# Four filler products for nine ahead of the third modulation unit, and the first weight difference moved behind a convolution

## What is computed

```python
mod = jax.nn.silu(c) @ w_ada[l] + b_ada[l]
shift1, scale1, gate1, shift2, scale2, gate2 = jnp.split(mod, N_MOD, axis=-1)
h = modulate(rmsnorm(x, norm1_w[l]), shift1, scale1)
proj = h @ w_in[l]
r_q, r_k, r_v, r_g, d_q, d_k, d_v, d_z, d_a, d_b = jnp.split(proj, cuts, axis=-1)
...
ret = rmsnorm(ret).reshape(B, T, RET_WIDTH) * jax.nn.silu(r_g.astype(jnp.float32))
qkv = jax.nn.silu(causal_dwconv(jnp.concatenate([d_q, d_k, d_v], axis=-1), conv_w[l]))
...
dn = gated_delta_rule(dq, dk, heads(cv, DN_HEADS), g, beta)
...
x = x + gate1[:, None, :] * mix
ffn = hierarchical_moe(h2, ...)
```

## Time and profile before

| | |
|---|---|
| three runs | 912.74, 915.47, 915.58 us (median 915.47) |
| the profiled execution | 915.49 us |
| its span, first to last instruction | 913.7 us |
| mean granted clock of PE | 0.994 of full speed |
| busy: PE, DVE, ACT, POOL | 98%, 46%, 36%, 13% |
| DMA over the span | 289.48 MB, 317 GB/s in the mean |

### The profile page before, as it was taken

The page is one execution under the profiler, slowest core; times in us unless marked ns, Lnnn a source line. Parts: engine busy times, 40 slices in busy tenths (PEclk is TensorE's granted clock), DMA queues, the critical chain, the costliest instruction groups (busy, mean ns, idle before and its releaser), DMA issues.

```text
span 913.7 us, 13676 instructions
## 1 busy us (share of the span) xinstructions
PE 897.8 (98%) x5638; PEld 584.3 (64%) x5638; DVE 417.2 (46%) x701; ACT 324.5 (36%) x522; POOL 114.9 (13%) x118
## 2 busy tenths in 40 slices
PE   9999999999999999999999999999998999999998
PEld 6798876777644434444344443444435899999886
DVE  2488535367422323222222232223234778888744
ACT  1376425333422222232122222222213555555531
POOL 1244472130000000000000000000000022222200
PEclk9999999999999999999999999999999999999999
DMA  9962269787999899999999999999999665555301
GB/s 364 418 283 93 93 227 362 265 351 292 378 420 388 343 420 420 422 419 422 418 421 419 420 422 420 421 419 420 421 420 357 214 195 179 180 182 184 131 1 47
DMA packets 60892, 289.48 MB, mean 317 GB/s; under 512 B 4500, under 2 KB 28692, under 8 KB 33688
## 3 DMA queue, kind: packets, MB, share of 16 engines
q1 hardware_dynamic: 59664, 285.38, 79.0%
q10 hardware_dynamic: 1160, 3.16, 0.9%
HBM read 287.47 MB, written 1.05 MB: 316 GB/s over the span
## 4 chain that ended last, share of the span: by engine, by line
PE 88%; DMA 3%; issue 3%; SPq 2%; POOL 2%; DVE 1%; ACT 1%; DVEq 0%; POOLq 0%; ACTq 0%
PE ps L1072 24%; PE ps L1096 12%; PE ps L556 9%; PE ps L1060 7%; PE ps L1193 7%; PE ps L1194 7%; PE ps L1195 7%; PE ps L1112 3%; DMA S<-in_ffn_cols_dram 3%; PE ps L1085 2%; PE ps L539 2%; PE ps L530 2%; PE ps L571 2%; PE ps L1177 1%; PE ps L546 1%
## 5 line engine op out<-in xcount | busy, mean ns | idle before, releaser
L1075 PE MATMUL ps<-ring,proj 128*64 128x512 f32 x320 | 140.9, 593 | 0.0
L1072 PE MATMUL ps<-ring,proj 128*64 128x512 f32 x304 | 133.9, 593 | 0.0
L1911 DVE TENSOR_TENSOR w_l<-ring,w_h 128x2048 fp32r<-128x2048 f32 x33 | 75.5, 2292 | 44.8 <-ACT w_h L2286 44.8
L1072 PEld LDWEIGHTS ps<-ring,proj 128*64 128x64 f32 x304 | 41.1, 137 | 84.6 <-issue 84.6
L1193 PE MATMUL ps<-h_h,w_h 128*128 128x256 f32 x336 | 95.1, 283 | 0.0
L1194 PE MATMUL ps<-h_l,w_h 128*128 128x256 f32 x336 | 95.1, 283 | 0.0
L1195 PE MATMUL ps<-h_h,w_l 128*128 128x256 f32 x336 | 95.1, 283 | 0.0
L2286 ACT CAST w_h<-ring 128x2048 fp32r<-128x2048 f32 x33 | 62.8, 1903 | 81.3 <-PE ps L1195 76.9
L1072 PE MATMUL ps<-arena,proj 128*64 128x512 f32 x208 | 91.6, 593 | 0.0
L1767 DVE SCALAR_TENSOR_TENSOR RQ<-ps,gate_of,proj 128x512 f32<-128x512 f32 x32 | 24.0, 751 | 147.1 <-PE ps L1097 147.1
L2242 ACT CAST MX_r<-RQ 64x512 fp32r<-64x512 f32 x62 | 38.2, 616 | 143.9 <-DVE RQ L1767 143.1
(11 more groups left out here) (394 smaller groups left out, 1666.7 us busy)
## 6 DMA issues: line engine op xcount, KB each, us to landing
ring<-in_w_dram SPq DMA_DIRECT2D x114, 1024.0 KB, 14.9
arena<-in_w_dram SPq DMA_DIRECT2D x72, 1024.0 KB, 15.9
ring<-in_ada_units_dram SPq DMA_DIRECT2D x11, 2048.0 KB, 8.7
ring<-in_ffn_w_in_dram SPq DMA_DIRECT2D x22, 1024.0 KB, 9.0
ring<-in_in_units_dram SPq DMA_DIRECT2D x6, 2048.0 KB, 19.7
ring<-in_ffn_w_out_dram SPq DMA_DIRECT2D x5, 2048.0 KB, 8.5
arena<-in_in_units_dram SPq DMA_DIRECT2D x2, 2048.0 KB, 30.1
ring<-in_out_units_dram SPq DMA_DIRECT2D x2, 2048.0 KB, 9.2
```

Source lines behind the costliest of these rows:

```text
L1072: pe.matmul(ps[0:SLOTS, :], XTe[i % 2][:, k, :], u1[:, k, :], start=(k == 0), stop=(k == 7))
L1075: t = pe.matmul(ps[64:64 + SLOTS, :], XTe[i % 2][:, k, :], u3[:, k, :], start=(k == 0), stop=(k == 7))
L1911: ve.tensor_tensor(low, src, dst.bitcast(F32), ALU.subtract).then_inc(split_ready, 1)
```

## The change

In the opening, the group of fillers between the column sums of unit 1 and ada(2) has four products in place of nine. On DVE, `lower(0)` is no longer run right behind the gates' reciprocal but in the second turn of the loop, behind `delta_conv(2, (2,))` and ahead of the queries' scaling.

```diff
             turn_over(2)
             column_total(0, 1, first)
-            turn_over(9)
+            turn_over(4)
             ada(2)
             turn_rows(0)
...
             ve.reciprocal(beta, ea).then_inc(*vd.up("gates"))
-            lower(0)
             for s, h4, c0 in ((1, slice(4, 8), 1.0), (2, slice(0, 4), 128.0 ** -0.5)):
                 if s == 2:
                     delta_conv(2, (2,))
+                    lower(0)
                 ve.wait_ge(qk_exp, s)
                 ve.scalar_tensor_tensor(qkv[:, h4, :], qkv[:, h4, :], c0, SQ[:, h4, :], ALU.mult,
```

## The result

| | before | changed |
|---|---|---|
| median of 20 runs each, us | 913.20 (910.13 to 915.58) | 915.22 (914.68 to 917.18) |
| ratio | | 1.0026, 95% interval 1.0017 to 1.0034 |
| span of the profiled execution, us | 913.7 | 913.2 |

The changed kernel is slower: by 2.0 us by the medians, by 2.4 by the ratio, whose interval reaches from 1.6 to 3.1 us. That is about 0.3%. The three times of before that stood ahead of the prediction lay high in what 20 runs show. Two runs were in a slow state and stand in no ratio: one of before, timed beside the experiments (2550.36 us), and one of e3 (1503.22 us, mean granted clock 0.556).

What follows compares the result with a forecast made beforehand. PE, busy 98% of the span, was taken as the bound. Opening -1.2, wait -1.66, clock -1.8, new wait +4.5 and clock again +1.8 summed to +1.6 us, 917.1; range 912.4 to 919.6.

Steps and rivals of the forecast that it cites:

- Opening, -1.2: Five fewer fillers before ada(2): transfer landings limit the gain to 1.2 us; ends 0 and 2.3.
- The wait before L690, -1.66: Gate sums: with lower(0) moved, POOL's four RQ copies run undisturbed and PE's 1.66 us wait goes.
- The clock behind it, -1.8: Behind L690: PE's clock fall to 0.50 goes along with the wait, saving 1.8 us.
- The new wait, +4.5: Before project(0): lower(0), in turn with POOL's subtractions, delays the fourth convolution and gate copy; PE waits 4.5 us.
- The clock behind the new wait, +1.8: From project(0)'s start: PE's clock falls behind the long wait, 1.8 us; ends 0 and twice that.
- What lies further down, 0: Behind project(0): DVE and POOL run 3.1 us late, but PE's masks are still done in time; cost 0.
- POOL never in the way: Rival at lower(0): POOL waits for it, PE waits 1.5 us and the clock holds; -3.1, 912.4 us, chance 0.06.
- DVE before POOL: Rival: query scaling follows lower(0) at once, POOL's subtraction after; PE waits 2.2 us; -0.7, 914.8, chance 0.09.
- the clock in the opening: Rival: with five fillers gone, the clock falls once between 20 and 34 us; +3.4, 918.9 us, chance 0.17.
- The clock holds behind the new wait: Rival at project(0): no clock fall behind the long wait; sum -0.2, 915.3 us, chance 0.09.

Runs made afterwards that it cites:

- e3: Changed kernel (four fillers) with lower(0) moved behind the copy of the gate sums: median 910.55 us, ratio to before 0.9973.
- e1: Changed kernel with lower(0) back behind the reciprocal, so four fillers alone against before: median 911.36 us, ratio to before 0.9994.
- e3n: Nine fillers as in before, lower(0) behind the copy of the gate sums: median 911.14 us, ratio to before 0.9969.
- e6: Six fillers, lower(0) behind the copy of the gate sums: median 910.87 us, ratio to before 0.9968.
- e2: Changed kernel with nine fillers again, so the move of lower(0) alone against before: median 916.77 us, ratio to before 1.0044.
- e5: Changed kernel with the products of the second "at" computed five times over, keeping PE busy in its wait: median 913.20 us, ratio to before 0.9996.
- e4: Changed kernel with POOL's two subtractions started only after DVE's query scaling: median 911.72 us, ratio to before 0.9992.
- the first four experiments: e1 to e4, each against before, timed in one group beside runs of before with median 912.64 us.

## Why the prediction was right

The forecast was +1.6 us and about even; measured were +2.0 to +2.4, by the chain of waits that was forecast. The forecast time of 917.1 was 1.9 too high, since it was reckoned from 915.47, and before's median in 20 runs is 913.20.

- **Opening, -1.2.** Measured in the changed kernel's profile -1.4 at the key projection (34.09 to 32.70) and -1.7 at the end of the delta projections (75.86 to 74.18), 0.2 to 0.5 more than forecast. The step held in this execution: the landings decide, not the products taken out (2.3). It does not hold in every one: where the clock was low at ada(0) (e1, e3n, e6), PE came after the landing and each product counted. The trace disagrees with the page of the Trainium skill on SBUF (SBUF — State Buffer, section "Summary: rules for kernel authors"), by whose 358 GB/s the transfer would have landed at 25.2, by estimate, and the opening would have given nothing: it landed at 3.08 + 19.5 = 22.58.
- **The wait before L690, -1.66.** Gone in the changed kernel and in every experiment that moves lower(0), with all four copies at 0.61. Held.
- **The clock behind it, -1.8.** For the one execution that was profiled it was 1.6 (20.31 against e1's 18.69), and even that isn't what the median pays. e1 has the same wait and no fall. So the medians of before hold a part of this 1.8 only, and the change could win only that part. This term was mis-sized: I took a chance event for a fixed cost.
- **The new wait, +4.5.** Measured 4.20 (L556 starts 10.17 behind L690, in e1 5.80, so PE is 4.4 late by it), with its parts as worked out: lower(0) 2.99 (2.9 forecast), query scaling 3.36 (3.4), released by DVE. The turn that POOL takes between DVE's two instructions, read from the feed-forward layer, came as read, in the changed kernel, e2 and e5 (that layer shows it 21 times, not 22: the last of its 22 is the L1925 without POOL). e4 shows that it is the cause of two thirds of the wait.
- **The clock behind the new wait, +1.8.** 2.9 in the changed kernel's profile, 1.3 in e2's, and 2.9 between the changed kernel and e5. It was charged too low: in the changed kernel the clock was low for most of the stretch from 83.9 to 91.0. The upper end of twice 1.8 covers it.
- **What lies further down, 0.** Held: DVE and POOL ran late and nobody waited for the masks. PE's lag is 2.26 at L539 (96.17 to 98.43) and still 2.25 at L955 (236.90 to 239.15).
- **The range.** The opening's clock at 918.9 with half a fall of 1.8 on top is 919.8, not 919.6.

By the terms as measured in the two profiles, -1.7 (opening) -1.7 (wait) -1.6 (clock) +4.4 (new wait) +2.9 (clock again), the sum to L539 is +2.3, and it is 98.43 - 96.17 = +2.26 (forecast +1.6). The medians say +2.0, the ratio +2.4. That all of them lie so close to the forecast is in part luck, since before's end holds chance events. Against before's 13 runs with a mean clock of 1.000 (median 910.99), the changed kernel's 13 at 0.996 (915.17) take 4.2 more, and the terms give +3.9 if before pays no fall. The forecast charged the clock too little at both places; that before's median pays for falls here and elsewhere brought the difference back to +2. Why the two spans say -0.5 shows in the clock further on, before and changed:

```profile
235.00:240.00 5.00, 4.13 (x27) 0.94 1.00 407
240.00:245.00 5.00, 5.00 (x34) 0.72 1.04 424
485.00:490.00 5.00, 2.76 (x17) 0.86 1.01 415
490.00:495.00 5.00, 5.00 (x29) 0.80 1.02 419
```

```profile
235.00:245.00 10.00, 9.14 (x62) 1.00 1.03 417
485.00:495.00 10.00, 7.99 (x54) 1.00 1.01 417
```

In the profiled execution of before the clock also fell around the start of the first expert (238.62) and behind the wait at 487.83; in the changed kernel's it did neither. From the rows the two falls cost 1.7 each (0.06 and 0.28 of five microseconds, 0.14 and 0.20). 2.26 less 3.4 is -1.1, against -0.5 of the spans; the rest was not traced. Of the rivals, "POOL never in the way" and "DVE before POOL" are refuted by the changed kernel's own rows, "the clock in the opening" by a clock of 1.00 from 20 to 34 us in all five profiles with four fillers. "The clock holds behind the new wait" is refuted by 0.53 from 83.9 to 91.0.

**The version to keep** is lower(0) behind the gate copy, with any of the three filler counts: 2.5 to 2.9 us under before by the ratios, 4.8 to 5.3 under the changed kernel by the same measure.

## What to carry to other kernels

Before a step is moved behind another, list what stands behind its new place in the same queue and who waits for each of those, banks to be freed among them: here the step moved was wanted late, but two small instructions behind it were wanted at once. A gap in which the engine waits for another one is the place for such a step. DVE instructions with both inputs in SBUF and POOL's took turns here (3.36 for a scaling that takes 1.22 with POOL moved away), so a move on DVE has to be laid beside POOL's timeline too; and where the shortened filler would end ahead of a landing, only the part up to the landing is won.

## What was not expected of the hardware

- The same wait of 1.66 us, in the same place, cost PE's clock in before's profile (0.50 from 79.0 to 82.4) and not in e1's (1.00 from 76 to 80). Behind the wait of 4.20 it fell in both profiles that have it, but for different lengths: project(0)'s first twelve matmuls took 5.26 and 4.16, at full clock 2.83. Behind 1.35 (e4) and with the wait filled (e5) it held.
- The clock at ada(0), ahead of everything that was changed, was 0.66 from 10 to 15 us in the profiles of e1, e3n and e6 and 1.00 in the six others. It decides whether PE or the transfer is late at ada(2).
- Before's runs spread over 5.5 us (910.13 to 915.58), the changed kernel's over 2.5 (914.68 to 917.18), whose mean granted clock was 0.993 to 0.996 in every one of its 20 runs. e2, with the same wait, had 0.994 to 0.996 in all its 8. Of before's runs beside the first four experiments, 13 had a mean clock of 1.000 (the run of 2550 us left out), and those lie from 910.0 to 911.4. The mean of a run doesn't say where its clock fell, so this is not shown but pointed to: with short waits the clock falls in some executions and not in others, with the long one it falls in all, and a single profile of a kernel with short waits says little on what its median pays for the clock.
